# Two small transformer blocks in one kernel: Ada rows by quarters, attention one chunk later, layer vectors and activations in another order

## The reference, cut to what matters

```
# block 1: bidirectional gated delta net, with modulation
mod = silu(c) @ w_ada + b_ada                # 6 x 1024: shift, scale, gate, twice; also for c_ctx
h   = rmsnorm(x, g) * (1 + scale) + shift    # x and context
u, z, q, k, v, b, g = short_conv(h @ w_in)   # q of x; k, v of both
x   = x + gate * rmsnorm(mixer_out(...), g)  # delta net in both directions, Fourier branch
x   = x + gate2 * rmsnorm(conv_ffn(modulate(rmsnorm(x))), g)   # up, 3x3 conv, silu, down
# block 2, two layers:
mod  = silu(c_2) @ ada_w + ada_b
h    = rms_norm(x, g) * (1 + sc_m) + sh_m
rq, rk, rv, rg, lx, ly, fq, fk, fv, ff, gates = split(h @ w_in)
ret  = silu(rg) * head_norm(retention(rope(rq), rope(rk), rv))
lru  = gelu(ly) * rg_lru(causal_conv(lx))
fox  = forgetting_attention(fq, fk, fv, log_sigmoid(ff + b_f))   # causal, 8 heads
x    = x + gt_m * rms_norm((sum of sigmoid(gate_i) * (branch_i @ w_o_i)) @ w_out, g)
x    = x + gt_f * rms_norm(square(relu(h @ w1)) @ w2, g)         # h modulated again; 1024 -> 4096 -> 1024
```

## Time and profile before

| what | value |
|---|---|
| median of three runs | 1972.3 us |
| profiled execution, in all | 1977.8 us |
| its span, first to last instruction | 1976.0 us |
| TensorE busy | 92% |
| VectorE, ScalarE, GpSimd busy | 59%, 40%, 2% |
| TensorE's granted clock, mean | 0.957 |
| DMA, mean | 167 GB/s |
| the stream's loads | 233 of 1 MB, median 4.8 us from issue to landing |
| Ada's slices by GpSimd | 64 of 1 MB, median 6.5 us |

### The profile page before, as it was taken

How to read it: one execution, slowest core, us unless ns; L and a number is a source line. 1 busy time by engine, 2 the same in 40 slices (tenths; PEclk the granted TensorE clock), 3 DMA queues, 4 the chain that set the end, 5 groups by cost and what they waited for, 6 DMA issues and landing times.

```text
span 1976.0 us, 33644 instructions
## 1 busy us (share of the span) xinstructions
PE 1816.4 (92%) x14788; PEld 1703.0 (86%) x14788; DVE 1171.7 (59%) x1479; ACT 790.7 (40%) x958; POOL 34.1 (2%) x68
## 2 busy tenths in 40 slices
PE   6896798887899998999999999998999999999998
PEld 4784697866699897999999989997999999979997
DVE  3464547544589836555787665455554687666453
ACT  3242121102433435354585444443544476444342
POOL 0001000010000000000000000000000000000000
PEclk7897799978899999999999999999999999999999
DMA  9677404152444443444455535552543454534552
GB/s 398 233 272 261 151 21 171 38 218 87 172 169 169 171 171 137 153 147 150 162 180 177 186 123 176 187 176 100 181 147 128 151 191 174 190 128 171 191 172 86
DMA packets 45205, 329.23 MB, mean 167 GB/s; under 512 B 5008, under 2 KB 5008, under 8 KB 5392
## 3 DMA queue, kind: packets, MB, share of 16 engines
q1 hardware_dynamic: 35712, 258.63, 37.2%
q0 software_dynamic: 9216, 67.11, 9.0%
q10 hardware_dynamic: 144, 1.51, 0.2%
HBM read 326.18 MB, written 1.05 MB: 166 GB/s over the span
## 4 chain that ended last, share of the span: by engine, by line
PE 71%; DVE 11%; ACT 7%; DMA 5%; issue 5%; SPq 0%; ACTq 0%; DVEq 0%; POOL 0%
PE ps L333 17%; PE ps L335 17%; PE ps L334 17%; DMA ada_raw<-ada 4%; ACT w_hi L929 4%; PE ps L386 4%; PE ps L599 3%; PE ps L458 2%; DVE w_lo L1381 2%; PE ps L611 2%; PE ps L437 2%; DMA ada<-ada 1%; PE ps L620 1%; DVE rstd L1419 1%; DVE rsq L2071 1%
## 5 line engine op out<-in xcount | busy, mean ns | idle before, releaser
L1381 DVE TENSOR_TENSOR w_lo<-raw,w_hi 128x2048 fp32r<-128x2048 f32 x211 | 483.3, 2292 | 512.5 <-ACT w_hi L929 512.0
L333 PE MATMUL ps<-act_hi,w_hi 128*128 128x256 f32 x2672 | 756.9, 283 | 24.9 <-DVE act_lo L1436 9.7
L334 PE MATMUL ps<-act_lo,w_hi 128*128 128x256 f32 x2672 | 746.0, 279 | 0.0
L335 PE MATMUL ps<-act_hi,w_lo 128*128 128x256 f32 x2672 | 746.0, 279 | 0.0
L929 ACT ACTIVATE w_hi<-raw 128x2048 fp32r<-128x2048 f32 (+1 forms) x233 | 428.7, 1841 | 563.9 <-PE ps L335 563.5
L333 PEld LDWEIGHTS ps<-act_hi,w_hi 128*128 128x128 f32 x2672 | 506.9, 190 | 36.5 <-issue 21.2
L334 PEld LDWEIGHTS ps<-act_lo,w_hi 128*128 128x128 f32 x2672 | 507.7, 190 | 0.9
L335 PEld LDWEIGHTS ps<-act_hi,w_lo 128*128 128x128 f32 x2672 | 505.9, 189 | 0.0
L333 PE MATMUL ps<-mlp_hi,w_hi 128*128 128x256 f32 x512 | 146.0, 285 | 8.5 <-DVE mlp_lo L2074 8.5
L334 PE MATMUL ps<-mlp_lo,w_hi 128*128 128x256 f32 x512 | 144.4, 282 | 0.0
L335 PE MATMUL ps<-mlp_hi,w_lo 128*128 128x256 f32 x512 | 144.3, 282 | 0.0
(11 more groups left out here) (389 smaller groups left out, 2270.8 us busy)
## 6 DMA issues: line engine op xcount, KB each, us to landing
raw<-stream SPq DMA_DIRECT2D x233, 1024.0 KB, 4.8
ada_raw<-ada POOLq DMA_DIRECT2D x64, 1024.0 KB, 6.5
ada_f<-ada SPq DMA_DIRECT2D x4, 1024.0 KB, 14.3
ada_a<-ada SPq DMA_DIRECT2D x3, 1024.0 KB, 19.5
consts_stage<-consts_a SPq DMA_DIRECT2D x1, 1728.0 KB, 32.6
consts_stage<-consts_b ACTq DMA_DIRECT2D x1, 1472.0 KB, 7.4
x<-xT SPq DMA_DIRECT2D x1, 1024.0 KB, 7.3
xc<-ctxT SPq DMA_DIRECT2D x1, 1024.0 KB, 9.4
```

The source lines that it names most:

```text
L333: mm(out, ah, bh, start=first, stop=False, skip_group_check=shared)
L334: mm(out, ah, bl, start=False, stop=False, skip_group_check=shared)
L335: return mm(out, al, bh, start=False, stop=last, skip_group_check=shared)
L1381: tt(w_lo[:, s2, :], raw[:, s4, :], w_hi[:, s2, :].bitcast(f32), ALU.subtract).then_inc(S("lo_ready"), 1)
```

## The change

Five edits, all of order:

1. The first Ada pairs give quarters of the rows: after each two slices ScalarE copies one bank, and the column matmuls of quarter 0 stand behind slice 3, of quarter 1 behind slice 5, of 2 and 3 behind slice 7.
2. Ada turns 0 and 1 move behind Q's second chunk and into the middle of the first KV chunk, and all turns up to 10 stand one place later; the last KV chunk writes banks 5 and 6; `ab_rows`, the context's modulation, small weights and `ada_rows(0)`, `ada_tr(0)`, `ada_out(0)` each move one or two chunks later; the strict wait ahead of UZ goes.
3. Attention's `fox_tr`, `fox_out`, `fox_split` and `rope` with its three VectorE steps go one chunk later.
4. Layer vectors and the next layer's first prep move ahead of `residual`, the second prep behind `modulate` on VectorE and behind the root on ScalarE.
5. In each MLP half the eighth activation goes ahead of the prep of the second deep chunk, which is done in halves; the first four activations stay a `job` (now unrolled), the others are written out.

```
+        KV_BANK = (2, 0, 2, 5)
@@ tensor
-            last.then_inc(S("mod_rows_mm"), 1)
-            pe.wait_ge(S("mod_rows_ev"), 1)
-            for c in range(2 * ADA_FIRST):
-                last = mm(ps[:, 5, 2 * c:2 * c + 2], mod_rows[:, c * P:(c + 1) * P], sel[:, 0:2], start=True, stop=True)
+                if m % 2 == 1:
+                    last.then_inc(S("mod_rows_mm"), 1)
+                for q in {3: (0,), 5: (1,), 7: (2, 3)}.get(m, ()):
+                    pe.wait_ge(S("mod_rows_ev"), q + 1)
+                    for c in range(4 * q, 4 * q + 4):
+                        last = mm(ps[:, 5, 2 * c:2 * c + 2], mod_rows[:, c * P:(c + 1) * P], sel[:, 0:2], start=True, stop=True)
             last.then_inc(S("mod_mm"), 1)
-            ada_mm(0)
-            ada_mm(1)
             begin(N_Q, 0)
             mod_chunk(N_Q % 2, 0, 1, 0).then_inc(S("chunk_done"), 1)
             job(feat_chunk, N_Q + 1, 1, 1, 1)
-            ada_mm(2)
-            pe.wait_ge(S("sw_wide"), 1)
-            pe.wait_ge(S("mod_lo"), 16)
-            small_mm(xc, 0)
-            small_mm(norm_h1, T).then_inc(S("ab_rows_mm"), 1)
+            ada_mm(0)
             for c in range(4):
                 n = N_KV + c
                 begin(n, n)
-                bank = n % 2 * 2
-                if c == 0:
-                    pe.wait_ge(S("evicted"), 2)
+                bank = KV_BANK[c]
                 feat_chunk(n % 2, bank + 1, 1)
                 if c == 0:
+                    ada_mm(1)
+                    pe.wait_ge(S("sw_wide"), 1)
+                    pe.wait_ge(S("mod_lo"), 16)
+                    small_mm(xc, 0)
+                    small_mm(norm_h1, T).then_inc(S("ab_rows_mm"), 1)
+                if c == 1:
                     pe.wait_ge(S("ab_rows"), 1)
                     small_tr(ab_rows, 4, 16).then_inc(S("ab_mm"), 1)
                 feat_chunk(n % 2, bank, 0).then_inc(S("chunk_done"), 1)
-                ada_mm(3 + c)
+                ada_mm(2 + c)
             for c in range(4):
-                job(feat_chunk, N_UZ + c, N_UZ + c, 1, 1, strict=c == 0)
-                if c == 1:
+                job(feat_chunk, N_UZ + c, N_UZ + c, 1, 1)
+                if c == 2:
                     ada_tr(0)
-                ada_mm(7 + c)
+                ada_mm(6 + c)
+            ada_mm(10)
...
-                group(tok_chunk, L_RV, 1, [lambda: fox_tr(0), lambda: fox_tr(4), fox_out, rope])
-                group(feat_chunk, L_LX, 1)
+                group(tok_chunk, L_RV, 1, [None, lambda: fox_tr(0), lambda: fox_tr(4), fox_out])
+                group(feat_chunk, L_LX, 1, [rope])
@@ scalar
+            def prep_halves(n):
+                act.wait_ge(S(f"raw_loaded{n % RAW}"), n // RAW * 16 + 16)
+                act.wait_ge(S("chunk_done"), n - 1)
+                act_(w_hi[:, n % 2, 0:CH // 2], raw[:, n % RAW, 0:CH // 2], ACT.Copy).then_inc(S("half_hi"), 1)
+                act_(w_hi[:, n % 2, CH // 2:CH], raw[:, n % RAW, CH // 2:CH], ACT.Copy).then_inc(S("hi_ready"), 1)
...
-            act_(mod_rows[:, :].rearrange("p (a b) -> p a b", a=4), ps[:, 1:5, :], ACT.Copy).then_inc(S("mod_rows_ev"), 1)
+            for q in range(4):
+                act.wait_ge(S("mod_rows_mm"), q + 1)
+                act_(mod_rows[:, q * 512:(q + 1) * 512], ps[:, 1 + q, :], ACT.Copy).then_inc(S("mod_rows_ev"), 1)
...
-            ada_rows(0)
             for c in range(1, 4):
                 job(N_UZ + c, N_UZ + c, 1, lambda i: flat(uz[:, 2 * (i + c):2 * (i + c) + 2, :]))
-                if c == 1:
+                if c == 2:
+                    ada_rows(0)
+                if c == 3:
                     ada_out(0)
...
+                elif c == 10:
+                    prep(N_LAYER, N_LAYER % RAW, N_LAYER % 2)
...
             root(4)
-            for n in (N_LAYER, N_LAYER + 1):
-                prep(n, n % RAW, n % 2)
+            prep(N_LAYER + 1, (N_LAYER + 1) % RAW, (N_LAYER + 1) % 2)
...
-                    job(n, j, 8, None, hook=mlp_steps)
+                    job(n, j, 4, None, hook=mlp_steps)
+                    for c in range(4, 7):
+                        prep(n + c + 2, (n + c + 2) % RAW, (n + c) % 2)
+                        mlp_steps(0, c)
+                    mlp_steps(0, 7)
+                    prep_halves(n + 9)
@@ vector
+            def prep_halves(n, e):
+                half = CH // 2
+                dve.wait_ge(S("half_hi"), e)
+                tt(w_lo[:, n % 2, 0:half], raw[:, n % RAW, 0:half], w_hi[:, n % 2, 0:half].bitcast(f32), ALU.subtract)
+                dve.wait_ge(S("hi_ready"), n + 1)
+                tt(w_lo[:, n % 2, half:CH], raw[:, n % RAW, half:CH], w_hi[:, n % 2, half:CH].bitcast(f32), ALU.subtract)\
+                    .then_inc(S("lo_ready"), 1)
...
             job(N_DOWN, 9)
+            layer_vectors(0)
+            prep(N_LAYER, N_LAYER % RAW, N_LAYER % 2)
             residual(4, 1, 2, y_down, gs[:, 2, :])
...
-                for n in (n0, n0 + 1):
-                    prep(n, n % RAW, n % 2)
                 modulate(ns, 3 + 2 * L, x, a5, gs[:, 0, :], mod[:, 0:8], act_hi[1], act_lo[1])
+                prep(n0 + 1, (n0 + 1) % RAW, (n0 + 1) % 2)
...
-                group(L_RV, [[], [], [], [lo_of(sp_ + 1, s4, 0)]])
-                group(L_LX, [[rope_sin], [rope_cos], [rope_add], []])
+                group(L_RV)
+                group(L_LX, [[lo_of(sp_ + 1, s4, 0)], [rope_sin], [rope_cos], [rope_add]])
...
+                if L + 1 < layers:
+                    layer_vectors(L + 1)
+                    prep(n0 + LAYER_CH, (n0 + LAYER_CH) % RAW, (n0 + LAYER_CH) % 2)
                 residual(ns + 3, 3 + 2 * L, 2, a5, gs[:, 2, :])
```

More of the change, by code:

```diff
@@ L1034, in _ @@
                     .then_inc(S("evicted"), 1)
-            act.wait_ge(S("ab_rows_mm"), 1)
-            act_(ab_rows[:, :], ps[:, 7, :], ACT.Copy).then_inc(S("ab_rows"), 1)
+                if c == 0:
+                    mod_hi(1, xc, None, act_hi[0])
             for c in range(4):
@@ L1039, in _ @@
                 prep(n + 2, (n + 2) % RAW, n % 2)
+                if c == 0:
+                    act.wait_ge(S("ab_rows_mm"), 1)
+                    act_(ab_rows[:, :], ps[:, 7, :], ACT.Copy).then_inc(S("ab_rows"), 1)
                 if c == 2:
@@ L1309, in _ @@
                 act.wait_ge(S("mods_done"), 4 + L)
-                group(L_RV, lambda c: vtok_r[:, :, c * T:(c + 1) * T], [lambda: fox_tr(0), lambda: fox_tr(4), fox_out, fox_split])
-                group(L_LX, to(s8))
+                group(L_RV, lambda c: vtok_r[:, :, c * T:(c + 1) * T], [None, lambda: fox_tr(0), lambda: fox_tr(4), fox_out])
+                group(L_LX, to(s8), [fox_split])
                 gate(L_RG, 0, keep=s3, after=[None, None, None, ret_out])
@@ L1361, in _ @@
                             sqrt_table()
+                        else:
+                            prep(m + 1, (m + 1) % RAW, (m + 1) % 2)
                         if hf == 1 and c % 2 == 1:
@@ L1364, in _ @@
                 root(ns + 3)
-                for m in (n0 + LAYER_CH, n0 + LAYER_CH + 1):
-                    prep(m, m % RAW, m % 2)
+                prep(n0 + LAYER_CH + 1, (n0 + LAYER_CH + 1) % RAW, (n0 + LAYER_CH + 1) % 2)
         @block.vector
@@ L1502, in _ @@
             prep(1, 1, 1)
+            nc.vector.memset(pre_kv[:, :, :, 0:T + 2:T + 1], 0.0).then_inc(S("pads"), 1)
+            nc.vector.memset(pre_q[:, :, 0:1], 0.0).then_inc(S("pads"), 1)
+            nc.vector.memset(pre_q[:, :, T + 1:T + 2], 0.0).then_inc(S("pads"), 1)
+            job(N_Q, 1)
             scale_shift(1, xc, gs[:, 0, :], mod_ctx[:, 0:8], act_hi[0], act_lo[0])
@@ L1507, in _ @@
                 .then_inc(S("sw_wide"), 1)
-            nc.vector.memset(pre_kv[:, :, :, 0:T + 2:T + 1], 0.0).then_inc(S("pads"), 1)
-            nc.vector.memset(pre_q[:, :, 0:1], 0.0).then_inc(S("pads"), 1)
-            nc.vector.memset(pre_q[:, :, T + 1:T + 2], 0.0).then_inc(S("pads"), 1)
-            job(N_Q, 2)
+            job(N_Q + 1, 1)
             def conv_q():
@@ L1560, in _ @@
                     conv_q()
-                    ab_part()
                 else:
                     conv_kv(c - 1)
+                if c == 1:
+                    ab_part()
                 if c == 2:
@@ L1807, in _, with layer_vectors @@
             up_lo(FB + 1, (FB - 1) % 2)
-            job(N_DOWN, 9)
-            residual(4, 1, 2, y_down, gs[:, 2, :])
-            for L in range(layers):
-                n0 = N_LAYER + L * LAYER_CH
-                j0 = J_LAYER + L * LAYER_J
-                ns, sp_ = 5 + 4 * L, 4 * L
+            def layer_vectors(L):
                 v = lambda name, n=1, i=0: V(name, n, i, L)
@@ L1827, in _ @@
                 order(stt(gs[:, 0, :], mod[:, 8:16], 1.0, v("g_pre_mix", KT), ALU.add, ALU.mult))
-                for n in (n0, n0 + 1):
-                    prep(n, n % RAW, n % 2)
+            job(N_DOWN, 9)
+            layer_vectors(0)
+            prep(N_LAYER, N_LAYER % RAW, N_LAYER % 2)
```

(17 more changed lines are left out.)

2 lines of the change are left out of this document (removed).

## The result

The changed kernel takes 1951.9 us (median of 4 runs, 1950.1 to 1955.1) beside 1973.4 for the kernel before on the same chip: a ratio of 0.9896 (95% interval 0.9875 to 0.9916). That is 21.4 us faster by the medians and 20.5 by the ratio. Predicted was 1946, range 1934 to 1961. Between the two profiled executions, span against span, it is 1976.0 less 1950.2, 25.8, where 26.4 was forecast. In a later series the changed kernel had 1951.5 (ratio 0.9882, 0.9862 to 0.9902). The experiments ran on three chips on which the kernel before has medians of 1972.0 (e1 to e4), 1968.9 (e5 to e8) and 1972.0 (f1 to f4), so between series the ratios are to be compared and not the medians.

The account below looks back on a forecast made before the run. TensorE, busy 92% of the span, bounds the kernel, the early part by transfers. Terms +2 - 7.8 - 11.4 - 9.2 = -26.4 turn 1977.8 into 1951.4, less 5.5 to the median: 1946 us, range 1934 to 1961.

Parts of the forecast that it names:

- the sum: Whole kernel: early part +2, attention -7.8, MLP -11.4, layer starts -9.2, together -26.4 us.
- MLP: MLP's last activation first: mlp_lo wait gone, gains 3.3, 1.7, 3.25, 3.2, in all -11.4 us (bounds -7, -13).
- Early part: Ada rows to Ada 12: last KV chunk 10.6 us early, Ada 12 late by 12.7, booked +2 (between -10 and +7).
- the layout: Behind the last KV chunk: step times in the old kernel's clock, from 126.3 to Ada 12's end at 201.3 us.
- the price of the slices: Behind the last KV chunk: slice landings, 5.1 to 9.5 us after issue, in the chain that gives back the 10.6.
- rival (a): Early part: slices land soon enough that the 10.6 us shift stays; -39, 1933 us; chance 0.12.
- Attention: Attention a chunk later: gain 5.6 at fox_tr, new wait 1.7 at ret_scores; net 3.9 a layer, -7.8 us.
- the forecast sign of 0.6 to 1 for w_lo: Second deep MLP chunk: TensorE would wait 0.6 to 1 us for w_lo, none for mlp_lo.
- the low clock to follow a gap of 2.25: TensorE: the 1.2 GHz clock follows gaps of 2.25, 3.6 and 4.1 us, but not one of 1.69.
- Layer starts: Both layer starts: rstd starts 3.4 us earlier, the second chunk's w_lo delays by some 0.7; -9.2 us (bounds -6, -11).

Follow-up runs that it names:

- e1: The changed kernel with the early part as before (Ada turns 0 and 1 ahead of Q, rows copied at once); 1947.9 us, ratio 0.9882.
- e4: The kernel before with only layer vectors and the w_lo of the layer's first chunk moved ahead of the residual; 1963.5 us, ratio 0.9951.
- e5: The changed kernel with ScalarE's square root for k and q ahead of its copy of Ada batch 1's rows; 1947.8 us, ratio 0.9896.
- e8: The changed kernel with the second deep MLP chunk's weights prepared whole instead of in halves; 1958.0 us, ratio 0.9943.
- f1: The changed kernel itself, unedited, run again to read the pace of chunks; 1951.5 us, ratio 0.9882.
- f4: The changed kernel with mended order, Ada turn 0 between Q's chunks, and rope_add right behind rope_cos on VectorE; 1930.6 us, ratio 0.9793.
- e6: The changed kernel with Ada turns, transposes and ScalarE's root and row copies reordered behind the last KV chunk; 1934.7 us, ratio 0.9820.
- e3: The kernel before with the MLP part alone (eighth activation ahead of the next chunk's preparation, this in halves); 1963.5 us, ratio 0.9957.
- e2: The kernel before with the attention part alone (fox_tr heads a chunk later, rope in LX, ret_scores behind rope_add); 1968.4 us, ratio 0.9979.

## Why the prediction was right

The range and the sign held, and the sum (-26.4) came within a microsecond of the profiled executions' -25.8. Part of that is luck. MLP moved 1.9 more than forecast, the other three terms together 2.4 less, and these errors cancel. And the execution of before from which the terms were read is a slow one (1977.8, where the 22 executions beside e1 to e4 lie between 1967.9 and 1978.4, median 1972.0): both the terms and the -25.8 contain what that execution lost beyond others.

**Early part: +2 forecast, +2.8 at DOWN's end in the two profiles, about 4 over all of them.** Last KV chunk 10.2 earlier (10.6), wait at `ada_tr(0)` 3.03 (3.1), Ada 12's end 4.0 later than before (2.1). The steps held, though not each time in them: the column matmuls end at 34.67, not 36.9, and Q starts at 40.13 instead of 41.7. The stretch behind went as laid out, the wait of 3.53 for w_lo ahead of UZ2 with it (147.4 to 150.8 in the layout). Missed was the low clock behind `ada_tr(0)`: Ada 8 took 3.64 instead of 1.9. I had taken the loss as the price of the slices. Most of it was the price of places in the order, as e6 shows: with another order DOWN ends 15 us earlier than before, where rival (a) asked for 10.6. But e6 also takes the root out of its place behind Ada's rows, which stood there in the kernel before too and was worth 5.3 at the norm in e5; how much of the 15 the early change brings is open.

**Attention: -7.8 forecast, -6.8 measured.** The wait at `fox_tr` is gone, the new one is 1.01, smaller than the 1.7 forecast. The gain in front of it was 4.4 a layer and not 5.6, because the four chunks from LX1 to RG0 run at the long pace, 0.8 us in all, and RG1 takes 0.3 more than its wait explains. No wait shows that.

**MLP: -11.4 forecast, -13.3 against this profile, -8.5 by the times of e3 (-5.5 to -11.2).** The term was mis-added: with waits of 0.6 to 1.0, two chunks take 11.9 to 12.3, which makes the gain 9.4 to 11.0 against the 58.56 of all four; the 1.7 booked at the second half should be 0.9 to 1.3 (from 13.21). `mlp_lo` is no longer waited for, as forecast. The wait for the halves is 0.3 in all, not 0.6 to 1.0 each: the whole chain from the relu ran earlier beside the chunk's end than I had it (halves ready at 1210.72, first deep chunk's end at 1211.04). So the forecast sign of 0.6 to 1 for w_lo did not show. The prediction took the low clock to follow a gap of 2.25; e4 shows full clock behind one of 2.32 and even one of 2.70, so the worth of this part differs from execution to execution.

**Layer starts: -9.2 forecast, -8.6 measured.** VectorE's and ScalarE's rows at the second one:

```profile
1344.62 1.75 DVE L1448 RECIPROCAL rstd<-std 128x256 f32<-128x256 f32 x1 [4.27 <-ACT std L977]
```
```profile
1344.12 0.47 ACT L977 ACTIVATE std<-ps,eps 128x256 f32<-128x256 f32 x1 [1.22 <-PE ps L438]
```

The reciprocal starts 0.03 after `std` ends (3.5 after in the earlier trace rows). TensorE's waits are 0.79 (0.7 forecast) and 0.73 to 0.80 for the second chunk's w_lo (0.7). The remaining 0.3 a start lies in the second chunk: it takes 6.46 and 6.53 instead of 5.44, of which the wait is 0.73 and 0.80. What the 0.3 is stays open.

**From the sum to the median.** I took the profiled execution to lie 5.5 above the median and subtracted that. The profile of after lay on its own median (1951.96 and 1951.93), so the 1946 came out 6 too low, 5.5 of it by this step. The step treated the offset of one execution as if it carried over to the other kernel. Put the other way, the medians moved 21.4 and not 26.4: one thing that the profile of before had more of than others is the low clock behind three of its four waits for `mlp_lo` (two in e2, none in e4). In the times of the single parts attention had -4.1 (forecast -7.8), MLP -8.5 (-11.4) and the layer starts -9.7 (-9.2).

## What to carry to other kernels

A wait on a transfer can be the order's fault: when a slot is filled only after its last use, ask at which place in the order the engine meets the slice, and put work between that doesn't need it. An engine that works through its list in order, and has a copy for one chain ahead of a step of another (ScalarE's rows ahead of the root), hands the first one's lateness to the second; look for such pairs before moving either. And compare single terms by stretches of the trace over several executions: differences of 2 to 4 us drown in a time of 1950.
